# Three gate chunks of a 1-core decoder kernel as seven block products, with their inputs stored away and brought back

## The reference

```python
xn = rmsnorm(x, norm_mix)
proj = xn @ w_in                      # columns: a_b, a_c, a_x, b_val, b_glu, q, gate_logits
...
ya, new_a = causal_dwconv(buf_a, a_c * a_x, conv_a_w)
ya = (a_b * ya) @ w_out_a
ub = b_val * jax.nn.sigmoid(b_glu)
yb, new_b = causal_dwconv(buf_b, ub, conv_b_w)          # width 31: the "taps"
yb = jax.nn.silu(layernorm(yb + conv_b_bias, ln_b_g, ln_b_b)) @ w_out_b
...                                                     # yx: cross attention
g = jax.nn.sigmoid(gate_logits + b_gate).reshape(bsz, t, N_BRANCH, D_MODEL)
merged = g[:, :, 0] * ya + g[:, :, 1] * yb + g[:, :, 2] * yx
h = x + merged @ w_o                                    # then a SwiGLU and a last norm
```

## Time and profile before

| | us |
|---|---|
| median of 3 runs | 1064.92 |
| lowest, highest | 1063.34, 1065.18 |
| the profiled execution, in all | 1064.31 |
| its span | 1062.4 |
| PE busy | 1051.5 (99%) |
| DVE busy | 764.7 (72%) |
| ACT busy | 489.2 (46%) |
| mean DMA rate | 175 GB/s |

### The profile page before, as it was taken

One profiled execution on the slowest core, in us unless ns is written; L12 is line 12 of the kernel. 1 busy time (PEld: TensorE's weight loads), 2 busy tenths in 40 slices (PEclk: granted clock), 3 DMA queues, 4 the chain that ended last, 5 costly groups with the idle time before them and its releaser, 6 DMA issues.

```text
span 1062.4 us, 20369 instructions
## 1 busy us (share of the span) xinstructions
PE 1051.5 (99%) x8703; PEld 1044.8 (98%) x8703; DVE 764.7 (72%) x1290; ACT 489.2 (46%) x560; POOL 114.5 (11%) x93
## 2 busy tenths in 40 slices
PE   9999999999999999999999999999999999999997
PEld 8999999999999999999999999999999999999996
DVE  6797888889888775686742855488777557688754
ACT  6745554544334353453446623344455245366432
POOL 4671000002300000000000000000000000000000
PEclk9999999999999999999999999999999999999999
DMA  8958787789787778668876653321687355487512
GB/s 299 293 172 198 170 214 195 221 211 306 234 242 160 198 198 181 176 156 197 199 188 158 172 203 117 98 82 48 158 214 169 118 140 140 126 201 181 158 40 81
DMA packets 155353, 186.19 MB, mean 175 GB/s; under 512 B 4822, under 2 KB 145454, under 8 KB 150262
## 3 DMA queue, kind: packets, MB, share of 16 engines
q1 hardware_dynamic: 121894, 106.64, 32.1%
q0 software_dynamic: 8496, 56.10, 26.6%
q10 hardware_dynamic: 24880, 22.26, 6.8%
HBM read 122.34 MB, written 7.54 MB: 122 GB/s over the span
## 4 chain that ended last, share of the span: by engine, by line
PE 90%; DMA 5%; POOL 1%; ACT 1%; DVE 1%; ACTq 0%; issue 0%; SPq 0%; DVEq 0%; POOLq 0%
PE acc L2436 38%; PE acc L2454 19%; PE acc L2860 11%; PE acc L2812 9%; PE acc L2819 5%; PE acc L2622 3%; DMA w_raw<-in_w_v_dram 2%; POOL w_l L776 1%; PE acc L2630 1%; DMA ws_l<-w_raw 1%; PE acc L2701 1%; PE acc L2408 1%; PE acc L2677 1%; DMA w_raw<-in_w_ff_gate_dram 1%; DMA w_raw<-in_w_ff_up_dram 1%; DMA w_raw<-in_w_k_dram 1%
## 5 line engine op out<-in xcount | busy, mean ns | idle before, releaser
L2436 PE MATMUL acc<-big_h,w_h 128*128 128x260 f32 x1536 | 310.8, 284 | 0.0
L2436 PE MATMUL acc<-big_l,w_h 128*128 128x260 f32 x1536 | 308.5, 282 | 0.0
L2436 PEld LDWEIGHTS acc<-big_h,w_h 128*128 128x128 f32 x1536 | 236.1, 188 | 0.5
L2436 PEld LDWEIGHTS acc<-big_l,w_h 128*128 128x128 f32 x1536 | 236.5, 188 | 0.0
L2454 PE MATMUL acc<-big_h,w_l 128*128 128x260 f32 x1536 | 193.0, 282 | 0.0
L2454 PEld LDWEIGHTS acc<-big_h,w_l 128*128 128x128 f32 x1536 | 188.1, 188 | 0.2 <-DMA w_l<-w_raw 0.2
L1573 DVE SCALAR_TENSOR_TENSOR ubyb<-ubyb,prm 128x512 f32<-128x512 f32 x240 | 180.3, 751 | 7.1
L807 ACT ACTIVATE w_h<-w_raw 128x1024 fp32r<-128x1024 f32 x112 | 112.2, 1052 | 95.3 <-DMA w_raw<-in_w_in_dram 29.5
L2812 PE MATMUL acc<-x_h,ws_h 128*128 128x260 f32 x504 | 125.9, 282 | 0.3 <-ACT cp L1299 0.2
L2812 PE MATMUL acc<-x_l,ws_h 128*128 128x260 f32 x504 | 125.7, 282 | 0.0
L2812 PEld LDWEIGHTS acc<-x_h,ws_h 128*128 128x128 f32 x504 | 94.8, 188 | 0.7 <-ACT cp L1299 0.7
(11 more groups left out here) (335 smaller groups left out, 1537.8 us busy)
## 6 DMA issues: line engine op xcount, KB each, us to landing
w_l<-w_raw POOLq DMA_DIRECT2D x37, 1024.0 KB, 8.1
w_raw<-in_w_in_dram SPq DMA_DIRECT2D x32, 1024.0 KB, 5.6
ws_l<-w_raw POOLq DMA_DIRECT2D x18, 768.0 KB, 6.5
w_raw<-in_w_ff_gate_dram SPq DMA_DIRECT2D x18, 512.0 KB, 5.3
w_raw<-in_w_ff_up_dram SPq DMA_DIRECT2D x18, 512.0 KB, 5.2
k_st<-in_cache_mem_k_dram ACTq DMA_DIRECT2D x8, 1024.0 KB, 9.0
v_st<-in_cache_mem_v_dram ACTq DMA_DIRECT2D x8, 1024.0 KB, 13.6
w_raw<-in_w_v_dram SPq DMA_DIRECT2D x4, 1024.0 KB, 8.5
```

The source lines that it names most:

```text
L2436: last = M.matmul(out[:, b, 0:HALF], w_h[:, slot, k, cols], xs[:, k_at + k, b * HALF:(b + 1) * HALF], start=start and k == 0 and xs is x[0 ...
```

## The change

`GLU_SEVEN`'s helpers are made general (`SEVENS` holds chunk numbers) and used for three gate chunks of A as well: C_A+2, C_A+4 and C_A+6. Their row sums are those of GLU: after GLU's first loads SP stores `tx_h`, `tx_l` in memory in four parts (`keep`), and brings them back during stage X (`bring_back`) to the place `ta` of the values' buffers. `ln_sum` and `uao` move to other places; `uao` now lies in that of `sg`, so the first sigmoid of A waits for its stores. The loops of stage A on PE and ACT are written out. The order of VectorE's taps changes in BA and A. The seven sums for the layer norm's mean stand together after the last gate chunk.

```diff
+SEVENS = (*(C_B + j for j in GLU_SEVEN), *range(C_A + 2, C_A + 8, 2))
...
+            def keep(n):
+                two_ = slice(n // 2 * 2, n // 2 * 2 + 2)
+                sp.wait_ge(t_lo, 4)
+                sp.dma_start(tx_dram[n % 2][:, two_, :, :], f(tx[n % 2][:, two_, :, :])).then_inc(t_kept, 16)
+            def bring_back(n):
+                two_ = slice(n // 2 * 2, n // 2 * 2 + 2)
+                sp.wait_ge(t_kept, 16 * 4)
+                sp.wait_ge(so_lo, NH)
+                sp.dma_start(f(ta[n % 2][:, two_, :, :]), tx_dram[n % 2][:, two_, :, :]).then_inc(t_back, 16)
             for j in range(8):
                 load(C_B + j, j % 2, win, (COL_BV if j % 2 else COL_BG) + j // 2 * CW)
+                if j >= 5:
+                    keep(j - 5)
             for j in range(4):
                 load(C_Q + j, j % 2, win, COL_Q + j * CW)
+                if j == 0:
+                    keep(3)
...
             for j in range(8):
                 load(C_X + j, j % 2, *((wox, j // 2 * CW) if j % 2 else (win, COL_GATE + BR_X * D + j // 2 * CW)))
+                if j >= 4:
+                    bring_back(j - 4)
...
+            def first_copy(c, u, quarter):
+                act.wait_ge(b_prod, 3 * nth(c) + 3)
+                if c % 2 == 0:
+                    act.wait_ge(acc_read, u)
+                nc.scalar.activation(quarter, acc[u % 4][:, 0, 0:HALF], ACT.Copy).then_inc(b_copy, 1)
...
             def out_t(h):
                 use = T[f"o{h}"]
                 done(use)
+                if h == 0:
+                    act.wait_ge(t_kept, 16 * 4)
...
-            gate_stage(T["a"], C_A, R_BG + BR_A, a_sig)
+            for it in range(4):
+                c, u0 = C_A + 2 * it, T["a"] + 4 * it
+                if it:
+                    first_copy(c, u0, quarters(0)[0])
+                split(c + 1, 1, u0 - 1)
+                if it == 0:
+                    act.wait_ge(uao_stored, 32)
+                elif it < 3:
+                    seven_minus(c + 2, u0 + 1)
+                for j in range(2):
+                    if it == 0:
+                        done(u0 + j)
+                        act.wait_ge(acc_read, u0)
+                        logits = halves(u0 + j)
+                    else:
+                        act.wait_ge(acc_read, u0 + 2)
+                        logits = two(sg[:, j, 2:SG])
+                    nc.scalar.activation(two(sg[:, j, 2:SG]), logits, ACT.Sigmoid, bias=param(2 * it + j, R_BG + BR_A)) \
+                        .then_inc(a_sig, 1)
+                if it == 3:
+                    split(C_GB, 0, u0 + 1)
+                else:
+                    if it == 0:
+                        seven_minus(c + 2, u0 + 1)
+                    blocks_hi(c + 2)
...
-                taps(4 if n % 2 else 3)
+                taps(4)
...
+            def sum_tiles():
+                dve.wait_ge(so_lo, NH)
+                dve.wait_ge(cs_step, KT)
+                dve.wait_ge(cv_step, KT * K_B)
+                for k in range(1, KT):
+                    V.tensor_tensor(ln_sum[:, :], ubyb[:, k, 0:TOK], ubyb[:, 0, 0:TOK] if k == 1 else ln_sum[:, :],
+                                    ALU.add).then_inc(ln_step, 1)
+                    if k < KT - 1:
+                        dve.wait_ge(ln_step, k)
             for it in range(4):
-                u0 = T["a"] + 4 * it
+                c, u0 = C_A + 2 * it, T["a"] + 4 * it
+                taps((6, 4, 4, 4)[it])
+                if it:
+                    first_sums(c, u0, quarters(0))
+                    taps((6, 6, KT * CV - made)[it - 1])
+                    last_sums(c, u0, quarters(0))
                 if it < 3:
-                    taps(((14, 5), (14, 4), (14, 4))[it][0])
+                    if it == 0:
+                        dve.wait_ge(ba_lo, KT)
+                    seven_sums(c + 2, 0, u0 + 1)
+                    seven_sums(c + 2, 1)
+                    sums_low(c + 2, 0)
+                    sums_low(c + 2, 1)
                 else:
-                    sum_first_tiles()
...
+                    sum_tiles()
                 dve.wait_ge(a_sig, 2 * it + 2)
                 for j in range(2):
...
-                        .then_inc(acc_read, 1 if j else 3)
+                        .then_inc(acc_read, 3 if it == 0 and j == 0 else 1)
                     if it < 3 and j == 0:
-                        taps(((14, 5), (14, 4), (14, 4))[it][1])
+                        taps((7, 4, 4)[it])
...
-            pairs(T["a"], C_A, (xn, br), (ba_lo, KT))
+            for j in range(8):
+                c, u = C_A + j, T["a"] + 2 * j
+                if j == 1:
+                    pe.wait_ge(ba_lo, KT)
+                if j == 2:
+                    pe.wait_ge(t_back, 16 * 4)
+                if c in SEVENS:
+                    seven_products(c, u, ta)
+                else:
+                    chunk(c, j % 2, u, u, (xn, br)[j % 2])
```

More of the change, by code:

```diff
@@ L65, with nth, halves_in, combs @@
 GLU_SEVEN = range(4, 8)
-def nth(j):
-    return j - GLU_SEVEN[0]
-def halves_in(j):
-    return 16 * (nth(j) // 2 + 1)
+SEVENS = (*(C_B + j for j in GLU_SEVEN), *range(C_A + 2, C_A + 8, 2))
+def nth(c):
+    return SEVENS.index(c)
+def halves_in(c):
+    return 16 * sum(n % 2 == c % 2 for n in SEVENS[:nth(c) + 1])
+def combs(c):
+    return sum(5 if n % 2 else 4 for n in SEVENS[:nth(c)])
 def ffn_order():
@@ L363, in decoder_step @@
     up_f = at("up_f", [P, 2 * TOK], f32, o)
+    uao = at("uao", [TS + 2, D], f32, o)
     p_f = at("p_f", [P, 4, N_MEM], f32, o)
@@ L601, in ob, with quarters @@
             return T[f"ob{n // 2}"] + n % 2
-        def glu_quarters(j):
+        def quarters(j):
             if j % 2:
@@ L988, in _ @@
                 else:
-                    glu_negative(n)
+                    seven_minus(C_B + n, T["b"] + 2 * n - 3)
                 if j in GLU_SEVEN:
-                    glu_copy(j)
+                    first_copy(C_B + j, T["b"] + 2 * j, quarters(j)[0])
                 if n in GLU_SEVEN:
-                    glu_hi_sums(n, 0)
-                    glu_hi_sums(n, 1)
-                    glu_hi_raw(n)
+                    blocks_hi(C_B + n)
                 if e % 2 == 0 and e in GLU_SEVEN:
@@ L1643, in glu_first, with last_sums @@
                 V.tensor_tensor(v, acc[(u + 1) % 4][:, 0, 0:HALF], u2, ALU.add).then_inc(b_uv, 1)
-            def combs(j):
-                return sum(5 if n % 2 else 4 for n in range(GLU_SEVEN[0], j))
-            def glu_combine(j):
-                u, k = T["b"] + 2 * j, nth(j)
-                c11, c12, c21, c22 = glu_quarters(j)
+            def last_sums(c, u, places):
+                k, before = nth(c), combs(c)
+                c11, c12, c21, c22 = places
                 P_, X, Y, Z = (acc[(u + n // 2) % 4][:, n % 2, 0:HALF] for n in range(4))
@@ L1682, in _ @@
                 if e in GLU_SEVEN:
-                    glu_combine(e)
+                    last_sums(C_B + e, T["b"] + 2 * e, quarters(e))
                     if e % 2:
@@ L1692, in _ @@
                 if n in GLU_SEVEN:
-                    glu_sums(n, 0)
+                    if n == GLU_SEVEN[0]:
+                        for s in range(2):
+                            dve.wait_ge(kv_stored[s], 16 * 4)
+                    seven_sums(C_B + n, 0, T["b"] + 2 * n - 3)
                 if j in GLU_SEVEN:
-                    glu_first(j)
+                    first_sums(C_B + j, T["b"] + 2 * j, quarters(j))
                 if n in GLU_SEVEN:
-                    glu_sums(n, 1)
-                    glu_low(n, 0)
-                    glu_low(n, 1)
+                    seven_sums(C_B + n, 1)
+                    sums_low(C_B + n, 0)
+                    sums_low(C_B + n, 1)
                 if j not in GLU_SEVEN:
@@ L1706, in _ @@
                 taps((0, 0, 8, 3, 2, 2, 2, 6)[j])
-            glu_combine(7)
+            last_sums(C_B + 7, T["b"] + 14, quarters(7))
             glu_product(7)
```

120 lines of the change are left out of this document (55 added, 65 removed).

## The result

The changed kernel takes 1069.33 us (median of 6 runs, 1067.5 to 1070.78); the kernel before, on the same chip, 1065.16 (6 runs, 1063.34 to 1066.98). The ratio is 1.0041, 95% interval 1.003 to 1.0053: slower, by 0.4%. The profiled execution took 1069.97 us, its span is 1068.2. The first lines answer to the earlier trace rows, the windows to the earlier trace rows.

The account below looks back on a forecast made before the run. TensorE was taken to bound the kernel, busy 1051.5 of 1062.4 us. The terms summed to +1.4 us, giving 1065.7 from the profiled execution or 1066.3 from the median; it said 1065.9, range 1063.0 to 1069.0.

Parts of the forecast that it names:

- Removed matmuls, free waits: Gate chunks C_A+2, +4, +6: 36 matmuls fewer, -4.31 us; banks freed earlier from the second on, -0.22 us.
- G1's copy and first sum: C_A+2: fifth product waits for ScalarE's copy, 1.35 us; sixth for VectorE's first sum, 1.48 us; together +2.83 us.
- G2 and G3: C_A+4 and C_A+6: copy costs nothing, sixth product 0.57 us late in each, together +1.14 us.
- `uao` and C_A+1: BA's taps make the copy of uao later, so C_A+1's split and low part come late: +0.75 us, bounds 0 and 1.5.
- Weight sums, layer norm's sums, the wait for `uao_stored`: Stage A: VectorE's added sums and the wait ahead of the first sigmoid are hidden and cost nothing.
- Storing: Four stores in GLU, DMA engines short of 3.6 us, first Q chunk's load late: +1.0 us, bounds 0 and 4.2.
- Bringing back: Four loads back in stage X push into neighbouring chunks, against slack of 2 to 3 us: +0.2 us, bounds 0 and 1.5.
- Rival 2: DMA bounds GLU and X; accumulates end behind load and store, from the second store on: 1068.3 us, chance 0.27.
- Rival 1: C_A+2's copy and first sum find VectorE earlier, the 3.97 us of waits go: 1061.7 us, chance 0.10.
- Rival 3: Edit of taps matters less, DMA all hidden: 1063.7 us; low end of the likeliest case (0.60), no chance of its own.

Follow-up runs that it names:

- third experiment: The changed kernel with VectorE's taps of stage A moved, none ahead of first_sums after the first iteration and 10 behind it; 1065.41 us, ratio 1.0002.
- moves only: The kernel before with only the eight transfers (four stores, four loads back) and their waits added, the data read by nobody; 1067.22 us, ratio 1.002.
- POOL's stores: The changed kernel with the four stores issued by POOL, each right behind the accumulating DMA of C_B+4 to C_B+7, not by SP; 1066.92 us, ratio 1.0023.
- one ahead: The changed kernel with three stores issued by POOL behind accumulates, the first still in SP's queue behind load C_B+5; 1070.71 us, ratio 1.0054.
- seventh experiment: The changed kernel with stores, loads back and taps at other places, plus 126 satisfied TensorE waits in A's block chunks; 1061.91 us, ratio 0.9972.

## Why the prediction was wrong, point by point
The forecast was 1065.9 us in 1063.0 to 1069.0; it came to 1069.33, beyond the range.

- **Removed matmuls, free waits** (-4.31, -0.22). Right: without the waits of G1 to G3 (third experiment) C_A+2 to +7 lasts 64.62 instead of 69.17 us, -4.55.
- **G1's copy and first sum** (+1.35, +1.48). Right in mechanism and size. The chain of the changed kernel:
```profile
488.94 5.47 DVE L1630 SCALAR_TENSOR_TENSOR ubyb<-ubyb,prm 128x512 f32<-128x512 f32 x7
```
```profile
496.28 0.39 PE L2685 MATMUL acc<-big_h,w_h 128*128 128x260 f32 x1 [1.01 <-ACT sg L1006]
```
```profile
495.05 0.70 DVE merged L2042
...
498.77 0.35 DVE sg L1696
499.12 0.04 issue
499.17 0.87 PE acc L2685 x5
```
  From start to start the two gaps are 1.29 and 1.45 us, less the pitch of 0.12: 1.17 and 1.33. G2 and G3 lost 0.37 each where 0.57 was said. Moving the taps took 3.7 us off these chunks.
- **`uao` and C_A+1** (+0.75). Right: the stage +0.76; with earlier taps in BA it fell to 24.23. That the size fits so well is in part luck: with the same taps it was +0.50 to +1.49 in the seven kernels, within the bounds.
- **Weight sums, layer norm's sums, the wait for `uao_stored`** (0). Right: no wait for them in any kernel.
- **Storing** (+1.0, bounds 0 to 4.2). Mis-sized, 2.7 in GLU and Q together, and the main failure. The step let the engines be "shared evenly", named the accumulates "within what they have" and charged the load of Q alone. Nothing was shared evenly: an accumulate moved no piece until 113 of a store's 128 had gone. It reckoned each transfer against its own slack and left out what ties them: the late accumulate holds back the next load, the late load meets the next accumulate, and ScalarE's negative waits for the load. Adding up the shares of the engines (30.8 + 12.8 = 43.6 of 40 us) also misled: the pieces of a store took 2.6 us of the 16 engines, less than the 3.2 charged, and the loss came all the same; with the stores behind the accumulates, a share of 0.99 cost nothing.
- **Bringing back** (+0.2, bounds 0 to 1.5). Measured +1.36, inside the bounds, but with the same code in SP's queue it was 0 in moves only and in POOL's stores, +0.14 in one ahead and +0.34 with the taps moved. Behind the odd loads it was 0 in all five kernels that had it there. In the changed kernel the accumulate issued at 381.28 landed 10.1 us later. Its first piece moved after 4.2 us, for the transfer back issued at 378.65 was still ahead of it. In moves only, POOL's stores, one ahead and taps moved the same accumulate moved its first piece after 1.4. What made the difference is the accumulate before it (364.57), which took 13.6 us where it was 10.8 to 11.5 in those four: so the next load and the transfer back behind it were issued 2 to 3 us later. Why that one took 13.6 us is open, so the 1.36 may be this execution's own.
- **Rival 2** (0.27, 1068.3) was the nearest. Its place, GLU first of all, and its size, 3.8 for the transfers against some 4.0, came true, the size by luck: it had 3.3 in GLU and 0.5 in X, and 2.7 (with Q) and 1.36 were measured. Its mechanism, that the accumulate always ends behind load and store by its smaller pieces, did not: with pieces of 1 KB GLU lost 3.7 us more, and what decided was what stood ahead. The loss also begins with the first store, not the second, and TensorE waited for `w_l` in one chunk of GLU, not in each. Rival 1 fell with G1. Rival 3's case, all hidden, is the ninth experiment's.
- **Feed-forward** (+1.25). Foreseen by nobody: no edit is near it. It came in every kernel with block products in A that was not padded; with 126 waits it went in one part of two in one kernel and all but 0.2 us in another, and with 168 in both. In the medians it is what is left: POOL's stores takes 1.8 us more than the kernel before, with GLU, Q, X and A as long as there or shorter and the feed-forward 1.5 longer. That a transfer of code inside the load goes with it is shown (0.9 us, 16 loads against 10), not how the rest of the code sets its place.

In the profiled executions storing, bringing back and the feed-forward are 1.7, 1.2 and 1.25 us beyond the forecast, and keys and values 0.6; the medians miss it by 3.4, so not all of this is in them.

What was wrong at the root: the price of a DMA was taken from its own duration, not from who waits for whom in the queue behind it.

## What to carry to other kernels
When a transfer is added beside a tuned stream of them, ask for each neighbour which transfer or engine waits for its landing, and follow that one step further; put the new one behind the transfer on which the next depends, in the queue that issues that, so that it fills the gap (behind it in another queue, it took turns with it here). The mean DMA share says little: 0.87 with the stores ahead lost 2.3 us, 0.99 with the stores behind none. Where block products take inputs through an in-order engine, keep long optional work behind the sums that the matrix engine waits for.

## What the runs showed of the hardware
- An accumulating DMA issued by POOL moved its first piece 1.4 us after its issue when nothing stood ahead. Behind a store of 1 MB it moved nothing until that was nearly done (issued 104.87, first piece 108.58, 113 of 128 pieces of the store gone; 943 of 1024 small ones, and 126 of 128, in two other kernels), and behind a load it was the same in the kernel before (issued 500.31, 923 pieces of the load and none of its own up to 505). In other stretches packets of two queues went one for one (64 and 65; 62 and 57).
- A store of 1.06 MB in 1024 pieces of 1040 bytes took 4.2 us of the 16 engines, in 128 pieces of 8320 bytes 2.6; the same edit cost 3.7 us of GLU, and 4.0 in Q, 1.5 of them by the clock.
- Code comes in transfers of 16 KB in one packet, 0.9 us at the least and 1.0 to 1.1 at the median. The second half (0.5 MB) of a load with one well inside took 10.2 to 10.4 us in 16 cases, without 9.2 to 9.4 in 10. Adding instructions to TensorE that do nothing moved them, and with them the waits of a stage 250 us later.
- A satisfied wait between matmuls costs nothing: 126 to 168 of them left the first pair of chunks with a block chunk at 21.63 us; the second pairs lost 0.5 us in the two kernels with 126, in one of them (the seventh experiment) in a wait for `w_l` whose accumulate, issued at 515.36, took 9.2 us, and none with 168.
- Behind a wait of TensorE of some 2 us the granted clock was 0.50 for 3.4 us in two executions (from 168.8 and from 197.6 us), and matmuls came 0.21 us apart instead of 0.12.
